# Indexer scores of a sparse-attention encoder layer: ScalarE only rectifies, VectorE weights and adds in one pass

## The reference, cut to what matters

```
rel = jax.nn.relu(jnp.einsum('btnd,bsd->btns', iq, ik))
score = jnp.einsum('btns,btn->bts', rel, iw)
...
score = jnp.where(admissible[None], score, -jnp.inf)
sel_score, sel = lax.top_k(score, topk)
```

## Time and profile before

| what | us |
|---|---|
| median of 3 runs | 3089.8 (3089.21 to 3094.53) |
| span of the profiled execution | 3078.3 |
| median less that span | 11.5 |
| TensorE busy, of the span | 2938.4 (95%) |
| VectorE busy | 1300.4 (42%) |
| ScalarE busy | 954.8 (31%) |
| GpSimd busy | 837.9 (27%) |

### The profile page before, as it was taken

The page is one execution under the profiler, slowest core; times in us unless marked ns, Lnnn a source line. Parts: engine busy times, 40 slices in busy tenths (PEclk is TensorE's granted clock), DMA queues, the critical chain, the costliest instruction groups (busy, mean ns, idle before and its releaser), DMA issues. The chain is left out here.

```text
span 3078.3 us, 46663 instructions
## 1 busy us (share of the span) xinstructions
PE 2938.4 (95%) x17655; PEld 2739.9 (89%) x17655; DVE 1300.4 (42%) x2804; ACT 954.8 (31%) x2297; POOL 837.9 (27%) x886
## 2 busy tenths in 40 slices
PE   4999999999999999999999989899999999999999
PEld 4766678889999899999999978799999999999998
DVE  6448986766424222222222255465241222222223
ACT  3355415555542211112111151377232111111110
POOL 7577710000022211112221067201222212211110
PEclk8999987899999999999999989899999999999999
DMA  4211240010120111111111023100101111111111
GB/s 137 64 44 54 76 152 25 27 36 27 34 85 28 42 42 41 41 41 41 54 55 41 14 60 102 61 28 9 42 28 56 55 42 42 52 46 42 42 42 59
DMA packets 90945, 154.54 MB, mean 50 GB/s; under 512 B 12240, under 2 KB 27472, under 8 KB 90640
## 3 DMA queue, kind: packets, MB, share of 16 engines
q1 hardware_dynamic: 72832, 128.74, 13.6%
q10 hardware_dynamic: 17936, 23.35, 2.2%
HBM read 127.13 MB, written 24.92 MB: 49 GB/s over the span
## 5 line engine op out<-in xcount | busy, mean ns | idle before, releaser
L797 PE MATMUL s_banks<-act_hi,ring_hi 128*128 128x352 f32 (+1 forms) x2496 | 825.3, 331 | 15.9 <-POOL ring_lo L1497 8.1
L799 PE MATMUL s_banks<-act_hi,ring_lo 128*128 128x352 f32 (+1 forms) x2496 | 818.4, 328 | 0.0
L798 PE MATMUL s_banks<-act_lo,ring_hi 128*128 128x352 f32 (+1 forms) x2496 | 817.9, 328 | 0.0
L1497 POOL TENSOR_TENSOR ring_lo<-raw,ring_hi 128x512 fp32r<-128x512 f32 x264 | 335.2, 1301 | 1223.0 <-ACT ring_hi L1327 1221.5
L797 PEld LDWEIGHTS s_banks<-act_hi,ring_hi 128*128 128x128 f32 x2496 | 471.4, 189 | 25.8 <-POOL ring_lo L1497 15.0
L798 PEld LDWEIGHTS s_banks<-act_lo,ring_hi 128*128 128x128 f32 x2496 | 473.3, 190 | 1.0 <-issue 0.3
L799 PEld LDWEIGHTS s_banks<-act_hi,ring_lo 128*128 128x128 f32 x2496 | 471.3, 189 | 0.0
L1886 DVE TENSOR_TENSOR silu_out<-silu_out,s_banks 128x384 f32<-128x384 f32 x132 | 70.2, 532 | 857.1 <-ACT silu_out L1341 857.0
L1897 DVE TENSOR_TENSOR xT<-xT,bank 128x352 f32<-128x352 f32 (+1 forms) x480 | 253.2, 532 | 191.9 <-PE bank L799 191.9
L797 PE MATMUL bank<-hT_hi,ring_hi 128*128 128x352 f32 (+1 forms) x960 | 313.6, 327 | 0.0
L799 PE MATMUL bank<-hT_hi,ring_lo 128*128 128x352 f32 (+1 forms) x960 | 313.6, 327 | 0.0
(11 more groups left out here) (161 smaller groups left out, 4403.4 us busy)
## 6 DMA issues: line engine op xcount, KB each, us to landing
raw<-in_w_up SPq DMA_DIRECT2D x176, 256.0 KB, 2.9
raw<-in_w_down SPq DMA_DIRECT2D x88, 256.0 KB, 3.5
raw<-in_w_even SPq DMA_DIRECT2D x40, 256.0 KB, 2.7
raw<-in_w_out SPq DMA_DIRECT2D x32, 256.0 KB, 2.9
scratch_cq<-p_out ACTq DMA_DIRECT2D x18, 256.0 KB, 2.0
q_tok<-scratch_cq SPq DMA_DIRECT2D x9, 512.0 KB, 3.4
xT<-in_xT SPq DMA_DIRECT2D x8, 544.0 KB, 5.2
out_yT<-xT SPq DMA_DIRECT2D x8, 544.0 KB, 2.7
```

Source lines behind the costliest of these rows:

```text
L797: pe.matmul(out, w_hi, x_hi, start=first, stop=False)
L798: pe.matmul(out, w_hi, x_lo, start=False, stop=False)
L799: return pe.matmul(out, w_lo, x_hi, start=False, stop=last)
L1497: pool.tensor_tensor(ring_lo[:, sl + k, :], raw[:, k % 4, :], ring_hi[:, sl + k, :].bitcast(F32), ALU.subtract).then_inc(lo_done, 1)
```

## The change: one VectorE pass a piece in place of two passes elsewhere

ScalarE keeps the rectifying pass, now into four buffers of `relu_o`, which take the room of `relu_w`. Its weighting pass goes, and so does GpSimd's adding pass. A new function of VectorE, `score_piece`, multiplies the rectified piece by the head's weight and adds it to the score in one instruction. VectorE does the pieces of unit u-1 at the head of its turn u, ahead of `sums(u)`.

```diff
-        relu_w = pr.cut("relu_w", [P, 2, 512])
-        relu_o = pr.cut("relu_o", [P, 2, 512])
+        relu_o = pr.cut("relu_o", [P, 4, 512])
...
                         act.wait_ge(piece_mm, i + 1)
-                        if i >= 2:
-                            act.wait_ge(piece_w, i - 1)
-                        act.activation(relu_o[:, i % 2, 0:w], bank(4 + i % 2)[:, 0:w], ACT.Relu).then_inc(piece_relu, 1)
-                        act.wait_ge(piece_relu, i + 1)
-                        if i >= 2:
-                            act.wait_ge(piece_add, i - 1)
-                        o = SCORE_OFF[tt] + c
-                        dst = relu_w[:, i % 2, 0:w] if h else score[:, o:o + w]
-                        act.activation(dst, relu_o[:, i % 2, 0:w], ACT.Copy,
-                                       scale=idx_w[:, tt, h:h + 1]).then_inc(piece_w, 1)
+                        if i >= 4:
+                            act.wait_ge(piece_add, i - 3)
+                        act.activation(relu_o[:, i % 4, 0:w], bank(4 + i % 2)[:, 0:w], ACT.Relu).then_inc(piece_relu, 1)
...
-                if layer == 0:
-                    for i in range(pieces_by(u - 1), pieces_by(u)):
-                        tt, h, c, w, _ = PIECES[i]
-                        pool.wait_ge(piece_w, i + 1)
-                        if i:
-                            pool.wait_ge(piece_add, i)
-                        o = SCORE_OFF[tt] + c
-                        if h:
-                            pool.tensor_tensor(score[:, o:o + w], score[:, o:o + w], relu_w[:, i % 2, 0:w],
-                                               ALU.add).then_inc(piece_add, 1)
...
+            def score_piece(i):
+                tt, h, c, w, _ = PIECES[i]
+                dve.wait_ge(piece_relu, i + 1)
+                if i:
+                    dve.wait_ge(piece_add, i)
+                sc, rl, wt = score[:, SCORE_OFF[tt] + c:SCORE_OFF[tt] + c + w], relu_o[:, i % 4, 0:w], idx_w[:, tt, h:h + 1]
+                if h:
+                    ins = dve.scalar_tensor_tensor(sc, rl, wt, sc, ALU.mult, ALU.add)
+                elif tt and c + w == score_width(tt):
+                    dve.tensor_scalar(sc[:, 0:w - P], rl[:, 0:w - P], wt, None, ALU.mult)
+                    ins = dve.scalar_tensor_tensor(sc[:, w - P:w], rl[:, w - P:w], wt, band_mask[:, 512:640],
+                                                   ALU.mult, ALU.add)
+                else:
+                    ins = dve.tensor_scalar(sc, rl, wt, None, ALU.mult)
+                ins.then_inc(piece_add, 1)
...
             for u in range(n_units):
                 if u < TILES and u % 3 == 0:
                     dve_token_mean(dve, layer, u // 3)
+                if layer == 0 and u:
+                    for i in range(pieces_by(u - 2), pieces_by(u - 1)):
+                        score_piece(i)
                 sums(u)
```

More of the change, by code:

```diff
@@ L456, in build @@
         piece_relu = sem("piece_relu")
-        piece_w = sem("piece_w")
         piece_add = sem("piece_add")
@@ L1764, in dve_project @@
             if layer == 0:
+                for i in range(pieces_by(n_units - 2), len(PIECES)):
+                    score_piece(i)
                 dve.wait_ge(topk_step, ITEMS_BY_UNIT[-1])
```

## The result

The changed kernel takes 3097.3 us against 3089.0 (medians of 14 runs each). The ratio over all runs, whose means are 3095.4 and 3088.7 us, is 1.0021, interval 1.0011 to 1.0031. That is 6.5 us slower, 3.4 to 9.6 with the interval. The forecast was 9.4 us.

What follows compares the result with a forecast made beforehand. VectorE and TensorE were taken as almost equally the bound from 214 to 434 us. New work 40 us, less 19.6 stalls, 8.2 waits and 2.8 head start, gave +9.4: 3089.8 to 3099.2 us, range 3085 to 3111.

Steps and rivals of the forecast that it cites:

- The new passes: 58 VectorE passes on score, pieces 38 to 95, with their waits for each other: 40 us of new work.
- What comes back: VectorE's small top-k steps no longer stalled by GpSimd's adds: 19.6 us back, bounds 10 to 27.8.
- The head start: Up to unit 22, TensorE's fourth piece no longer waits behind ScalarE's weighting pass: 2.8 us saved.
- The waits filled: VectorE's waits for squares and a matmul between 214 and 434 us vanish under new work: 8.2 us.
- starts late enough to stay the later one to the end: Behind unit 40, TensorE needs 5.5 us a unit, VectorE a little less, yet VectorE still ends last.
- the other way of the loop: Rectify waits for VectorE's passes, TensorE's piece for the rectify: 8.3 against 12.1 us, 3.8 to spare, VectorE never waits.
- Cheap passes: Rival: new passes at the one-input price, 26 us in all, giving -4.6 us, 3085; chance 12%.
- The second blocking: Rival: GpSimd's subtractions hold about 17 new passes for some 0.57 us each, +10 us, 3109; chance 14%.
- All stalls gone: Rival: stalls by GpSimd's subtractions vanish too, another 8.2 us back, +1.2 us, 3091; chance 14%.
- The clock: Rival: TensorE idles more and its clock halves in all 15 units or so, up to 3140 us; chance 5%.
- the 11.5 us between span and median: Runs shown exceed the profiled span by 11.5 us, added on both sides of the change.
- the attention simply shifts: Behind the projection, the later end of the stretch passes on in full to the attention.

Runs made afterwards that it cites:

- e5_halves: Changed kernel, but a VectorE pass waits for the last pass on the same columns, not the pass in front; ratio to before 1.0003.
- e1_no_adds: Kernel before with GpSimd's adds of heads 1 to 7 left out, no new passes; ratio to before 0.9982.
- e3_early: Kernel before with VectorE's one pass for pieces 0 to 37 only, the rest as before; ratio to before 0.9986.
- e4_late: Kernel before with VectorE's one pass for pieces 38 to 95 only, the earlier ones as before; ratio to before 1.0052.
- e7_table_before: Kernel before with the top-k item table charged for the new passes, so items move to the attention; ratio to before 1.0051.
- f2_after_again: Changed kernel, nothing altered, in a second profiled execution; 3091.3 us.
- e6_table: Changed kernel with the top-k item table charged for the new passes, moving 82 items to the attention; ratio to before 1.0030.

## Why the prediction was right, step by step

**The new passes: right.** Forecast 40 us. The rows by shape give 37.9 us with their gaps for 52 of the passes; the other passes (those of head 0, with the mask) add 3.9, and the first and last of a turn overlap their neighbours by about 2. The term came out right because the prices of the two-input rows held to 0.01 us. What I called the wait, 4.4 us of gaps, is only part of what waiting costs: `e5_halves` shows some 7, the overlap included.

**What comes back: right.** 43 x (0.406 - 0.292) + 31 x (0.501 - 0.162) + 32 x (0.370 - 0.232) = 19.8 us, where 19.6 was forecast; the stalls by `ring_lo` stayed. `e1_no_adds` shows the same means without any passes, so this term is the adds' alone.

**The head start: right for the trace that it was read from, too small for most.** 2.66 us for 2.8 in the first pair, and 2.4 in `e3_early` alone. But the first profile of before is an exception here. From the first matmul of unit 12 to the first count, before and then its second execution:

```profile
110.49:215.87 105.38, 98.83 (x403) 67.24 (x402) 39.58 (x67) 52.42 (x105) 67.06 (x85) 1.00 0.13 38
```

```profile
111.36:218.43 107.07, 100.54 (x403) 68.55 (x402) 39.60 (x66) 52.39 (x105) 67.00 (x85) 0.98 0.12 37
```

The three other kernels whose first pieces go the old way (`e1_no_adds`, `e4_late`, `e7_table_before`) take 106.9 to 107.0 us like the second, and all nine executions in which they go the new way 102.2 to 102.4. Each of the four longer ones has one stretch of 3.4 us at half clock between 180 and 204 us; the first profile of before and the nine have none. So the head start is 3.1 us against the execution that the sum was read from, and 4.7 against the other four; in the second pair the first count comes 5.6 us earlier, 0.9 of them there before unit 12. The term that was mis-sized is this one: 2.8 us counts the saved weighting passes, and not the stretch of low clock that four of these five executions have. Why the clock never fell there with the new form is not shown.

**The waits filled: nearly right.** In the first profile VectorE still waits 1.6 us, so 6.6 are filled and not 8.2. With the terms as measured the sum is 41.8 - 2 - 19.8 - 6.6 - 2.7 = +10.7, and the trace shows +10.8. In the second pair VectorE waits 9.6 us from its first count on before, and nothing but 0.2 us after:

```profile
DVE head_ss L1693 <- ACT p_sq L1182: 9.0, 11, 2.9
DVE p_out L1721 <- PE s_banks L881: 0.6, 1, 0.6
```

```profile
DVE count_flags L1632 <- DVEq L1697: 0.2, 1, 0.2
```

With 20.0 for the passes less the stalls, as in the first pair, the sum there is 20.0 - 9.6 - 5.6 = +4.8, and the trace shows +4.6. That the forecast of 9.4 comes near the 10.8 of the first pair is in part luck: its before happened to be the one execution with no low clock ahead of the first count.

The step that failed is that VectorE "starts late enough to stay the later one to the end": it does so in `f2_after_again` (72.53 us behind unit 41), and not in the first profile, where TensorE ended last again.

What makes TensorE late there is the other way of the loop that I had priced as harmless. VectorE hardly waits through it, as forecast; but TensorE does, for `relu_o`, longer than before: 29.1 us of weight loads against 22.3 (24.8 against 23.1 in the second executions). The row of before, 214 to 446 us:

```profile
PEld bank L859 <- ACT relu_o L1216: 22.3, 22, 2.1
```

In the longest of these tails the clock fell to half. Unit 39's matmuls took 7.96 us instead of 5.73, unit 41 started late, and VectorE caught up.

**The rivals.** Cheap passes: no, by the rows. The second blocking: not here, but in `e6_table`. All stalls gone: no, `enough` and `take` kept theirs. The clock: it did fall more often, as that rival had it, for 17 us instead of 3.5 in the first pair and 20 instead of 7 in the second. In the second execution VectorE waits 0.2 us in spite of it, so it cost the stretch nothing there; in the first the 1.6 us of waits left are what can be seen of it in the sum. In `e3_early`, where TensorE is the bound, two more such stretches took 3.2 us.

**Beside the sum.** I read the 11.5 us between span and median as lying around the span. The runs show only some 1.8 us there (3096.8 of time for the span of 3095.0); the rest is scatter between executions, and the profiled one of before was a short one. As it was added on both sides, the forecast doesn't suffer. That the attention simply shifts held in the first pair, 458.0 us before and 456.3 after. In the second it is 458.1 and 451.4, with 75 and 62 us at half clock. The chances of slower add up to 64 and not to 62; 59 was taken.

Open is how more counts in the first attention make the clock fall for longer. That moving the items lengthens the attention is shown by `e7_table_before`, which differs from before in the table alone; that it is by the clock, and not by VectorE's work itself, is argued from how the two go together, and no run separates them.

## What to carry to other kernels

Count what an engine gets back in waits that others forced on it before calling it full: here half of the new work was paid for by stalls beside GpSimd's adds. Then look at who ends last behind the stretch, because work given back to an engine that isn't the bound only becomes another wait (`e1_no_adds`). And if work moves onto an engine that also does deferrable work, move some of that too, and look at what its new place pays: half the charge, with the shorter chain, won where the whole one lost, though no run separates the two.

## What the runs showed that I had not expected

A wait for the instruction just in front on the same engine costs more than the gap that it shows: 0.105 us of gap and 0.08 of overlap between two passes, some 7 us in the stretch. In the projection from 214 us on, a unit whose matmuls lie under 3.4 us of low clock takes 1.6 us longer, 7.34 instead of 5.74. And moving VectorE's items by a few us changed what GpSimd's subtraction meets: in `e6_table` the passes of 320 columns take 0.705 us on the mean, not 0.549, and `enough` 0.445 and not 0.292, while `take` is down to 0.159 from 0.232.
